# A chunked recurrence in a decoder step: full 128x128 products per head against pairs of 64x64 products over six heads

## The reference

```python
def step(S, inp):
    r_t, w_t, k_t, v_t, a_t, b_t = inp
    sa = jnp.einsum('bhij,bhj->bhi', S, a_t)
    S = S * w_t[:, :, None, :] + sa[..., None] * b_t[:, :, None, :] + v_t[..., None] * k_t[:, :, None, :]
    return S, jnp.einsum('bhij,bhj->bhi', S, r_t)

S_T, ys = lax.scan(step, wkv_prev.astype(jnp.float32), xs)
```

## Time and profile before

| | us |
|---|---|
| median of three runs | 2152.48 |
| lowest, highest of them | 2148.63, 2153.54 |
| profiled execution, first to last instruction (span) | 2149.3 |

### The profile page before, as it was taken

One profiled execution on the slowest core, in us unless ns is written; L12 is line 12 of the kernel. 1 busy time (PEld: TensorE's weight loads), 2 busy tenths in 40 slices (PEclk: granted clock), 3 DMA queues, 4 the chain that ended last, 5 costly groups with the idle time before them and its releaser, 6 DMA issues. The chain is left out here.

```text
span 2149.3 us, 36383 instructions
## 1 busy us (share of the span) xinstructions
PE 1997.6 (93%) x13436; PEld 1752.8 (82%) x13436; DVE 1071.0 (50%) x2312; ACT 605.2 (28%) x1443; POOL 328.5 (15%) x651
## 2 busy tenths in 40 slices
PE   5999989989999659999999897999999999999997
PEld 5999965656666327989985597999999999999996
DVE  5333336754555485566543533553545545545555
ACT  5121224532323334545432432111111111111113
POOL 1000022334444034131310121000000000000000
PEclk8999999989999769999986798999999999999999
DMA  7111113025555100000003211112111121020202
GB/s 233 44 42 49 28 61 73 23 66 152 147 154 148 32 0 2 2 2 2 2 16 111 63 30 30 45 30 64 30 46 53 30 60 41 29 69 16 68 19 104
DMA packets 148250, 119.07 MB, mean 55 GB/s; under 512 B 22900, under 2 KB 136298, under 8 KB 147805
## 3 DMA queue, kind: packets, MB, share of 16 engines
q1 hardware_dynamic: 138189, 97.45, 15.5%
q0 software_dynamic: 9744, 18.78, 3.1%
q10 hardware_dynamic: 144, 0.52, 0.1%
HBM read 102.90 MB, written 11.44 MB: 53 GB/s over the span
## 5 line engine op out<-in xcount | busy, mean ns | idle before, releaser
L200 PE MATMUL bank<-normed2T_hi,w_hi 128*128 128x384 f32 (+1 forms) x1056 | 346.1, 328 | 4.3 <-DVE w_lo L490 4.3
L202 PE MATMUL bank<-normed2T_lo,w_hi 128*128 128x384 f32 (+1 forms) x1056 | 345.7, 327 | 0.0
L201 PE MATMUL bank<-normed2T_hi,w_lo 128*128 128x384 f32 (+1 forms) x1056 | 345.7, 327 | 0.0
L200 PEld LDWEIGHTS bank<-normed2T_hi,w_hi 128*128 128x128 f32 x1056 | 199.1, 189 | 5.5 <-DVE w_lo L490 5.5
L201 PEld LDWEIGHTS bank<-normed2T_hi,w_lo 128*128 128x128 f32 x1056 | 199.1, 189 | 0.0
L202 PEld LDWEIGHTS bank<-normed2T_lo,w_hi 128*128 128x128 f32 x1056 | 199.0, 188 | 0.0
L490 DVE TENSOR_TENSOR w_lo<-work,w_hi 128x1024 fp32r<-128x1024 f32 (+2 forms) x120 | 118.6, 990 | 131.4 <-ACT w_hi L485 130.2
L200 PE MATMUL bank<-inner_hi,w_hi 128*128 128x384 f32 (+1 forms) x528 | 174.5, 330 | 10.2 <-DVE w_lo L490 7.1
L202 PE MATMUL bank<-inner_lo,w_hi 128*128 128x384 f32 (+1 forms) x528 | 173.9, 329 | 0.0
L201 PE MATMUL bank<-inner_hi,w_lo 128*128 128x384 f32 (+1 forms) x528 | 173.7, 329 | 0.0
L200 PE MATMUL bank<-normedT_hi,w_hi 128*128 128x384 f32 (+3 forms) x480 | 158.0, 329 | 5.6 <-DVE w_lo L490 5.6
(11 more groups left out here) (473 smaller groups left out, 3954.8 us busy)
## 6 DMA issues: line engine op xcount, KB each, us to landing
work<-in_w_up_dram SPq DMA_DIRECT2D x44, 512.0 KB, 3.9
residualT<-in_cache_kv_latent_dram SPq DMA_DIRECT2D x80, 128.0 KB, 2.4
residualT<-in_cache_kv_latent_dram POOLq DMA_DIRECT2D x80, 128.0 KB, 2.6
work<-in_w_in_dram SPq DMA_DIRECT2D x19, 512.0 KB, 3.8
work<-in_w_down_dram SPq DMA_DIRECT2D x32, 256.0 KB, 2.9
weight_ring<-in_cache_kv_latent_dram POOLq DMA_DIRECT2D x48, 128.0 KB, 2.7
weight_ring<-in_cache_kv_latent_dram SPq DMA_DIRECT2D x48, 128.0 KB, 2.4
residualT<-residual_spill SPq DMA_DIRECT2D x1, 4352.0 KB, 16.7
```

What stands on the lines that cost most here:

```text
L200: pe.matmul(out, w[0], x[0], start=first, stop=False)
L201: pe.matmul(out, w[1], x[0], start=False, stop=False)
L202: return pe.matmul(out, w[0], x[1], start=False, stop=last)
```

## The change

Only the recurrence changes.

- One head's two chunks are now two 64x64 matrices, chunk 0 on partitions 0 to 63 and chunk 1 on partitions 64 to 127, beside each other for six heads: a tile [128, 6, 64]. A product of all six heads and both chunks is twelve products 64x64x64 (`by_chunk`), alternating between two quadrants of TensorE's array, into one bank. NQ, MP and AP have 128 columns instead of 64.
- One instruction copies out one bank, 384 columns of six heads (for NQ, NN, MP, RT and G several of 192 or 384 columns from two banks). `take_dve` and `take_act` have about 30 operations a tile in place of 105.
- N and its transpose come from two sets of products (NQ, NN) in place of the transpose NT; the powers of both are kept. The inverse's own transpose is made by TT. RT, G, HS and YV write the two chunks to two banks. HS and YV leave their sums open in their banks, and CH and S add the state's share there, so that no copy lies between.
- Tiles are solved in pairs, tile a in one set of buffers and banks 0 to 3, tile b in the other and banks 4 to 7. `levels` lists ten levels of a tile; a pair runs level 1 of a, level 1 of b, level 2 of a, and so on. The bank of each operation comes from a ring of four per tile, and the wait for it from `rw_freed`.
- GpSimd does one instruction a tile (`start_inverse`, N plus the unit matrix); the zero-padded copies are gone.
- The sample's tile is opened in the prompt's block and solved alone, in seven levels. In the sample's products behind it 64 columns take the place of 128.
- The table of constants has 1516 columns in place of 1708.

The core of the diff (removed functions are those printed above):

```diff
+        class Strand:
+
+            def __init__(self, take):
+                def heads(w):
+                    return take(H * w).rearrange("p (h w) -> p h w", h=H)
+
+                self.nat_b, self.nat_k, self.nat_v = (take(AW) for _ in range(3))
+                self.am, self.oq, self.mp, self.wu = (heads(P) for _ in range(4))
+                self.nd, self.ndt, self.n2, self.n2t = (heads(HD) for _ in range(4))
+                self.t, self.off, self.tt, self.u = (heads(HD) for _ in range(4))
+                self.n4, self.n4t, self.n8t = self.nd, self.ndt, self.n2
+                self.rt, self.gts = (take(2 * 3 * HD).rearrange("p (c m t) -> p c m t", c=2, m=3) for _ in range(2))
+
+        cw = Carve(loop_base)
+        strands = [Strand(rr), Strand(cw.take)]
+        states = sT[:, 9, 0:768].rearrange("p (s m v) -> p s m v", s=4, m=3)
...
+        def opening(i):
+            return [(i, "nat", 3), (i, "NQ", 0), (i, "NN", 0)]
+
+        def levels(i):
+
+            if i == NPT_:
+                return [[(i, "MP", 0), (i, "P2", 0), (i, "P2", 1)], [(i, "T2", 0), (i, "P4", 1), (i, "MV", 0)],
+                        [(i, "nat", 0), (i, "T4", 0)], [(i, "nat", 1), (i, "TT", 0)], [(i, "nat", 2)],
+                        [(i, "AP", 0), (i, "AP", 1)], [(i, "RT", 0)]]
+            return [[(i, "MP", 0), (i, "P2", 0), (i, "P2", 1)],
+                    [(i, "T2", 0), (i, "P4", 0), (i, "P4", 1), (i, "MV", 0)],
+                    [(i, "T4", 0), (i, "P8", 0)], [(i, "T8", 0), (i, "nat", 0)], [(i, "YT", 0), (i, "TT", 0)],
+                    [(i, "H1", 0), (i, "nat", 1)], [(i, "H2", 0), (i, "nat", 2)], [(i, "H3", 0)],
+                    [(i, "AP", 0), (i, "AP", 1)], [(i, "RT", 0), (i, "G", 0)]]
+
+        def joins(i):
+            return [(i, "YV", 0), (i, "HS", 0)]
+
+        prompt_ops = opening(0) + opening(1)
+        for a in range(0, NPT_, 2):
+            b = a + 1
+            for of_a, of_b in zip(levels(a), levels(b)):
+                prompt_ops += of_a + of_b
+            following = opening(a + 2)
+            prompt_ops += joins(a) + [(a, "CH", 0)] + joins(b) + [(a, "S", 0), (a, "S", 1), (a, "CH", 1)]
+            prompt_ops += following[:2] + [(b, "CH", 0)] + following[2:] + [(b, "S", 0), (b, "S", 1), (b, "CH", 1)]
+            if b + 2 < NPT_:
+                prompt_ops += opening(b + 2)
+        sample_ops = [o for level in levels(NPT_) for o in level]
+        all_ops = prompt_ops + sample_ops
...
+        def op(i, what, k=0):
+            return number[i, what, k]
+
+        ON_DVE = {"NQ", "NN", "MP", "T2", "T4", "T8", "H1", "H2", "H3", "RT", "G", "CH"}
+        IN_PLACE = {"CH": "HS", "S": "YV"}
+        TWO_BANKS = {"NQ", "NN", "MP", "RT", "G", "HS", "YV"}
...
+        rw_bank, rw_freed, ring, holder = {}, {}, [0, 0], {}
+        for n, (i, what, k) in enumerate(all_ops):
+            if what in IN_PLACE:
+                first = number[i, IN_PLACE[what], 0]
+                rw_bank[n], rw_freed[n] = [rw_bank[first][k]], []
+                holder[rw_bank[n][0]] = n
+                continue
+            s = i % 2
+            rw_bank[n] = [4 * s + (ring[s] + j) % 4 for j in range(2 if what in TWO_BANKS else 1)]
+            ring[s] += len(rw_bank[n])
+            rw_freed[n] = sorted({holder[b] for b in rw_bank[n] if b in holder})
+            for b in rw_bank[n]:
+                holder[b] = n
...
+        def products(pe, ops):
+            for i, what, k in ops:
+                n = op(i, what, k)
+                for earlier in rw_freed[n]:
+                    taken(pe, earlier)
+                product_of(pe, i, what, k, [PS[b] for b in rw_bank[n]]).then_inc(rw_mm, 1)
+
+        def by_chunk(pe, bank, left, right):
+
+            for h in range(H):
+                for c in range(2):
+                    r = rows_c(c)
+                    last = pe.matmul(bank[r, h * HD:(h + 1) * HD], left[r, h, 0:HD], right(r, h), start=True,
+                                     stop=True, skip_group_check=True)
+            return last
+
...
+            if what in ("NQ", "MP"):
+                for m in range(3):
+                    for f in range(2):
+                        for c in range(2):
+                            r, t = rows_c(f), slice(HD * c, HD * c + HD)
+                            x = sT[r, m + (3 if what == "MP" else 0), i * P + HD * c:i * P + HD * c + HD]
+                            last = pe.matmul(banks[f][rows_c(c), m * P:(m + 1) * P].rearrange("p (w t) -> p w t", w=2),
+                                             x, AR[r, m, i, :, t], start=True, stop=True, skip_group_check=True)
...
+            if what == "NN":
+                for m in range(3):
+                    for f in range(2):
+                        for c in range(2):
+                            r, t = rows_c(f), slice(HD * c, HD * c + HD)
+                            x = sT[r, m, i * P + HD * c:i * P + HD * c + HD]
...
+            for f in range(2):
+                taken(pe, op(i, "AP", f))
+            if what == "G":
+                taken(pe, op(i, "nat", 1))
+            if what == "HS":
+                taken(pe, op(i, "nat", 2))
+            for m in range(3):
+                for part in range(1 if what in ("RT", "G") else 2):
+                    for c in range(2):
+                        for f in range(2):
+                            r, h = rows_c(c), 2 * m + f
+                            cols = slice(h * HD, (h + 1) * HD)
+                            left, right = {
+                                ("RT", 0): (z.wu[r, h, 0:HD], z.oq[r, h, HD:P]),
+                                ("G", 0): (z.wu[r, h, 0:HD], z.nat_b[r, cols]),
+                                ("HS", 0): (z.nat_b[r, cols], z.wu[r, h, HD:P]),
+                                ("HS", 1): (z.nat_k[r, cols], z.nat_v[r, cols]),
+                                ("YV", 0): (z.wu[r, h, HD:P], z.oq[r, h, HD:P]),
+                                ("YV", 1): (z.nat_v[r, cols], z.mp[r, h, HD:P])}[what, part]
+                            last = pe.matmul(banks[c][rows_c(f), m * HD:(m + 1) * HD], left, right,
+                                             start=(m == 0 and part == 0), stop=what in ("RT", "G"),
+                                             skip_group_check=True)
+            return last
...
+                if what == "NQ":
+                    for f in range(2):
+                        dve.tensor_tensor(of_parity(z.ndt, f), by3(b[f], P)[:, :, 0:HD], mask("diag_t" + mk, HD),
+                                          ALU.mult)
+                    for f in range(2):
+                        ins = dve.tensor_tensor(of_parity(z.oq, f), by3(b[f], P), mask("off_keep" + mk, P), ALU.mult)
+                elif what == "NN":
+                    for f in range(2):
+                        ins = dve.tensor_tensor(of_parity(z.nd, f), by3(b[f], HD), mask("diag_n" + mk, HD), ALU.mult)
+                elif what == "MP":
+                    for f in range(2):
+                        ins = dve.tensor_tensor(of_parity(z.mp, f), by3(b[f], P), mask("keep" + mk, P), ALU.mult)
                 elif what in ("T2", "T4", "T8"):
-                    ins = dve.tensor_tensor(tinv[:, h], b[:, 0:P], tinv[:, h], ALU.add)
-                elif what in ("H1", "H2"):
-                    ins = dve.tensor_tensor(buf(h, PA)[:, 0:P], b[:, 0:P], buf(h, XX)[:, 0:P], ALU.add)
-                elif what == "H3":
-                    ins = dve.tensor_tensor(buf(h, XX)[:, 0:P], b[:, 0:P], buf(h, XX)[:, 0:P], ALU.add)
+                    ins = dve.tensor_tensor(z.t, flat, z.t, ALU.add)
+                elif what in ("H1", "H2", "H3"):
+                    ins = dve.tensor_tensor(z.u, flat, z.tt, ALU.add)
+                elif what == "P2":
+                    ins = dve.tensor_copy(z.n2t, flat)
+                elif what == "P4":
+                    ins = dve.tensor_copy(z.n4t, flat)
+                elif what == "AP":
+                    ins = dve.tensor_copy(z.wu[:, 0:3], by3(b[0], P))
...
+                        ins = dve.tensor_tensor(z.rt[:, c], by3(b[c], HD), AR[:, :, i, 1, HD * c:HD * c + HD],
+                                                ALU.add)
+                elif what == "G":
+                    for c in range(2):
+                        ins = dve.tensor_tensor(z.gts[:, c], by3(b[c], HD), mask("eye2", HD), ALU.add)
                 else:
-                    q = 2 * i + h
...
+                    q = 2 * i + k
+                    ins = dve.tensor_tensor(states[:, (q + 1) % 4], by3(b[0], HD),
+                                            dc[:, :, q:q + 1].broadcast_to([P, 3, HD]), ALU.mult)
...
+                if what == "S":
+                    ins = nc.scalar.copy(AR[:, :, i, 0, HD * k:HD * k + HD],
+                                         b[:, 0:3 * HD].rearrange("p (m t) -> p m t", m=3))
+                elif what == "AP":
+                    ins = nc.scalar.copy(z.wu[:, 3:6], b[:, 0:3 * P].rearrange("p (h w) -> p h w", h=3))
```

(66 more changed lines are left out.)

357 lines of the change are left out of this document (95 added, 262 removed).

## The result

The changed kernel takes 2030.8 us (median of 4 runs, 2028.91 to 2032.99), the kernel before beside it 2152.08 (4 runs, 2148.63 to 2153.54): ratio 0.9438, 95% interval 0.9425 to 0.9452. The profiled execution took 2032.99 us, its span is 2031.3.

A forecast was written before the change was run, and what follows sets the result against it. Bound by TensorE at about 23.5 us a prompt tile; savings of 89.6 (block), 4.5, 1.5 and 0.3 sum to 95.9 us, so the span goes from 2149.3 to 2053.4, plus 3.2 gives 2057 us, range 2032 to 2108.

The forecast's parts named there:

- A diagonal record: In the prompt's tiles, a 64x64x64 product alternating between two diagonal quadrants costs 30 ns, low end 27.
- A: Rival: in the prompt's block TensorE's queue sets the pace, 48 ns a record, about 2132 us; chance 0.12.
- B: Rival: in the prompt's block small products take their own time whichever quadrant, 59 ns each, about 2217 us; chance 0.04.
- C: Rival: TensorE's clock falls in the prompt's block; at half clock 45.4 us a tile, about 2236 us; chance 0.04.
- D: Rival: copies become the bound of the prompt's block; VectorE's were put at 10.9 of 23.5 us a tile.
- The cover by the second tile: In a pair, the other tile's level hides handovers of 0.91 us (ScalarE 0.83), leaving 0.1 us stall a tile.
- the sample's handovers: In the sample's solve, without a second tile: waits of 0.9, 0.3, 0.2 and 0.8 us, last copies 1.1.
- the cost of a record outside the diagonal groups: In the prompt's tiles: 55 ns for NQ and MP (128 columns), 30 ns for NN, RT, G, HS and YV.
- 23.5: TensorE's time for one prompt tile in us, 16.6 + 4.0 + 1.3 + 1.1 + 0.4 + 0.1, against 34.4 before.
- The waits: About 80 semaphore waits a prompt tile on TensorE's queue, taken at 0.4 us, from 0 to 2.5.
- Start, end and the sample's opening: Parts of the prompt's block beside its eight tiles: 3.7, 1.5 and 2.7 us, together 7.9.
- The sample's solve: The sample's tile solved alone after the prompt's block: 13.6 us against 19.3; of 5.7 saved, 4.5 taken.

The follow-up runs named there:

- e3: Changed kernel with the two tiles of a pair solved one after the other instead of interleaved by level: 2076.24 us.
- e4: Changed kernel with each copy of 384 columns after `by_chunk`, and that of `nat` 0, split into six of 64: 2033.73 us.
- e5: Changed kernel with the products of RT and G issued twice in the prompt's tiles: 2045.47 us.
- e6: Changed kernel with RT and G merged into one product of 128 columns, 24 records a tile fewer: 2026.4 us.
- e9: Changed kernel with RT and G of the prompt's tiles given their right-hand columns twice, same records; computes wrong values, only timed: 2034.38 us.
- e8: Changed kernel with about 500 more semaphore waits, satisfied long before, on TensorE's queue: 2039.55 us.
- e11: Changed kernel without the 493 of 697 TensorE waits that an earlier wait covers: 2026.97 us.
- e2: Changed kernel with RT, G, HS, YV, NQ, MP and NN issued as diagonal pairs of quadrants: 2035.07 us.

## Why the prediction was wrong in size

**Right.** A diagonal record costs 29 ns (30 taken), and keeps that pace for hundreds of records: A at 48 ns and B at 59 are refuted as prices of the block. The clock stayed at 1.00 (C), even with TensorE 22% idle in e3. The other engines are hidden (D): VectorE 62 of 140 us, and still hidden at 78 in e4. The cover by the second tile holds, with no stall ahead of most levels and 45 us lost without it (e3); alone, the sample's handovers show at about the forecast size. An addition of 384 columns is 0.56 us on VectorE; GpSimd's takes 1.00 us, not 1.4, and is hidden.

**The step that failed** is the cost of a record outside the diagonal groups: "their quadrants come in the order of f and c, so some neighbours share rows of the array", 55 ns for `NQ` and `MP`, and 30 ns for `NN`, `RT`, `G`, `HS` and `YV`. Measured are 27 and 16: products on four different quadrants are in flight together. The two rows used as bounds had two halves or two quadrants in turn, and nothing in the trace of before visits four. Per tile that is 48 x 28 ns + 168 x 14 ns = 3.7 us less, and 0.4 less for 29 instead of 30 ns: 23.5 would become 19.4.

**What took part of it back** is what the prediction had only as rival A, a queue that sets the pace. It doesn't at 30 ns a record, but at 15 it does: TensorE is idle for 10.4 of 140 us (129.57 busy), 1.6 us a tile, of which 0.3 are waits for the state's copy. 19.4 + 1.6 = 21.0 against 21.65 measured; 0.6 us a tile I can't assign. That instructions are what is missing is seen in the packets, at every stand, and in five runs: records cost 26 to 38 ns where their array time is 15 (e5), removing them gives back 23 to 34 ns each with the columns unchanged (e6), doubling the columns costs almost nothing (e9), and even waits have a price (e8, e11). The waits were costed at 0.4 us a tile with an upper end of 2.5; 493 of them in 8 tiles and the sample are worth 4 to 6 us, 0.5 to 0.7 a tile.

**Smaller terms.** Start, end and the sample's opening take 177.2 - 4 x 43.3 = 4 us where 7.9 were taken; the opening is `NQ` and `NN`, four-quadrant groups. The sample's solve is 12.5 instead of 13.6 (its terms add to 13.5), and `MP` and `RT`, four-quadrant groups too, explain 1.0 of that. The profiled time stood 1.7 us above its span, not 3.2, and the median 2.2 below that time. The block saved 18.7 us more than forecast, the other parts 3.4, and these two make 3.7: with rounding, the 26 us between 2057 and 2030.8.

**The Trainium skill** says in "TensorE: Matmul & The Clock Gate", section "Wait — 56ns, not 53.3ns?", that a product's start-to-start distance doesn't go under about 25 ns. The diagonal groups (29 ns) agree; the four-quadrant groups with 64 columns, at 15 to 16 ns a record, don't, and the measurement decides. Taken as a floor on every record, it would have kept me from the right sum too. "TensorEngine Tiling (Array Packing)", section "Key Properties", has tiles of the array working independently of each other, which the four quadrants bear out.

**What stays open** is what keeps the next packet: in the stretch shown it sets off 1.6 to 1.8 us after the first instruction of the one ahead of it, and is in use 1.3 us after its landing. No run moved a packet in time. Also open are the 0.6 us a tile, and why a wait instruction costs more (18 to 33 ns) than the 15 ns of its place in a packet.

## What to carry over

Count the instructions of a kernel of small products as well as their array time: a 64x64 product over all four quadrants leaves a record every 15 to 16 ns, but instructions came in for one every 30, 256 at a time, so that wider products (one of 128 columns for two of 64) and fewer waits gained what another order of quadrants did not. Where an engine stands with nothing to wait for, count the instructions from stand to stand and look at the instruction queue at these times. Interleaving two independent tiles was worth 45 us and hid the copies, however they were cut, so look for the saving at the copies last. When bounding an unseen cost, ask which resource the nearest rows held fixed (here: two quadrants), and let the low end go below them.

## What the runs showed of the chip

- Records of 64x64 fp32 products in four different quadrants come 15 to 16 ns apart with 64 columns and 27 with 128; in two diagonal quadrants 29 and 55.
- Products for a free quadrant ran while those of an earlier pair of quadrants were still in flight: 18 to 23 ns a record in groups issued pair by pair (e2).
- TensorE's instructions came in packets of 256 (16 KB), one fetched ahead. A packet was in use 1.2 us after its landing at the earliest, and from one stand to the next a packet took 3.8 to 4.1 us (after, six times), so TensorE stood for up to 1.4 us in the middle of a group once records came faster than about one in 30 ns. Slower array work in front shortened the stand (e9: 1.28 to 0.41 us).
- A semaphore wait cost 8 to 17 ns on the average (e8, e11), 18 to 33 for each wait instruction that is left in the queue, and nothing in the half of a pair at array pace, though its record is 51 ns long.
- TensorE's clock stayed at 1.00 with products that use a quarter of the array each, and with 22% of the time idle (e3).
